# Attention scores as three products of split operands, with one scaling moved from VectorE to ScalarE

## What is computed

```python
o_a = natten_latent(qa, ka, va, ka_c, va_c, rpb_a[l])    # 8 heads of 64, with a bias, "A"
o_b = swa_latent(qb, kb, vb, kb_c, vb_c, sink_b[l])      # 12 heads of 64, banded, with a sink, "B"
o_c = mla_latent(qc, kc, vc, kc_c, vc_c)                 # 6 heads of 128+64, dense, "C"
x = x + gate * merge_out(o_a, o_b, o_c, z, w_out[l])
if not last:                                             # layer 0 only: the context stream
    oa_c, ob_c, oc_c = ctx_attn(...), ctx_attn(...), ctx_attn(...)
    xc = xc + gate_c * merge_out(oa_c, ob_c, oc_c, z_c, w_out[l])
```

## Time and profile before

| | |
|---|---|
| median of three runs | 3156.88 us (3156.69 to 3157.13) |
| the profiled execution | 3160.49 us, its span 3159.2 us |
| TensorE busy | 3093.2 us (98%) |
| VectorE busy | 1893.5 us (60%) |
| ScalarE busy | 1340.6 us (42%) |
| GpSimd busy | 295.6 us (9%) |
| attention of layer 0 | about 692 to 850 us |
| attention of layer 1 | about 1488 to 1584 us |

### The profile page before, as it was taken

How to read it: one execution, slowest core, us unless ns; L and a number is a source line. 1 busy time by engine, 2 the same in 40 slices (tenths; PEclk the granted TensorE clock), 3 DMA queues, 4 the chain that set the end, 5 groups by cost and what they waited for, 6 DMA issues and landing times.

```text
span 3159.2 us, 51244 instructions
## 1 busy us (share of the span) xinstructions
PE 3093.2 (98%) x21274; PEld 2759.7 (87%) x21274; DVE 1893.5 (60%) x2949; ACT 1340.6 (42%) x2075; POOL 295.6 (9%) x386
## 2 busy tenths in 40 slices
PE   7999999999999999998999999999999999999998
PEld 3788888875688898886599999999999999999998
DVE  4376676377768566446757755555556555555445
ACT  4422333355532643345544444344444444444443
POOL 0001000017421010002710000000000000000000
PEclk9999999999999999999999999999999999999999
DMA  9776554221166387432064555555554555555554
GB/s 398 290 236 217 180 192 161 79 74 67 41 253 220 121 300 245 154 112 103 31 204 167 180 184 186 185 190 194 191 193 166 199 194 194 193 195 194 194 194 160
DMA packets 154984, 571.27 MB, mean 181 GB/s; under 512 B 17760, under 2 KB 17888, under 8 KB 152192
## 3 DMA queue, kind: packets, MB, share of 16 engines
q1 hardware_dynamic: 147312, 533.71, 49.2%
q0 software_dynamic: 7440, 34.28, 3.0%
HBM read 555.34 MB, written 12.58 MB: 180 GB/s over the span
## 4 chain that ended last, share of the span: by engine, by line
PE 92%; DVE 2%; DMA 2%; ACT 2%; issue 1%; POOL 1%; SPq 0%; DVEq 0%; ACTq 0%
PE ps L908 20%; PE ps L910 20%; PE ps L909 20%; PE ps L897 7%; PE ps L899 7%; PE ps L898 7%; DMA sb_raw<-in_stream 2%; PE ps L1081 2%; PE ps L1039 1%; PE ps L1062 1%; PE ps L817 1%; PE ps L1055 1%; POOL sb_p L2258 1%; PE ps L1030 1%; DVE sb_p L1982 1%
## 5 line engine op out<-in xcount | busy, mean ns | idle before, releaser
L1566 DVE TENSOR_TENSOR sb_wlo<-sb_raw,sb_whi 128x1024 fp32r<-128x1024 f32 (+1 forms) x809 | 983.5, 1217 | 974.9 <-ACT sb_whi L1151 973.3
L1151 ACT ACTIVATE sb_whi<-sb_raw 128x1024 fp32r<-128x1024 f32 (+1 forms) x813 | 853.9, 1051 | 1030.5 <-PE ps L910 781.0
L908 PE MATMUL ps<-sb_hn_hi,sb_whi 128*128 128x256 f32 (+4 forms) x2944 | 822.3, 279 | 4.4 <-DVE sb_hn_lo L1680 4.4
L909 PE MATMUL ps<-sb_hn_lo,sb_whi 128*128 128x256 f32 (+4 forms) x2944 | 820.9, 279 | 0.0
L910 PE MATMUL ps<-sb_hn_hi,sb_wlo 128*128 128x256 f32 (+4 forms) x2944 | 820.7, 279 | 0.0
L908 PEld LDWEIGHTS ps<-sb_hn_hi,sb_whi 128*128 128x128 f32 x2944 | 555.1, 189 | 5.2 <-DVE sb_hn_lo L1680 4.6
L910 PEld LDWEIGHTS ps<-sb_hn_hi,sb_wlo 128*128 128x128 f32 x2944 | 555.5, 189 | 0.0
L909 PEld LDWEIGHTS ps<-sb_hn_lo,sb_whi 128*128 128x128 f32 x2944 | 555.3, 189 | 0.0
L899 PE MATMUL ps<-sb_whi,sb_lo 128*128 128x512 f32 (+1 forms) x968 | 376.4, 389 | 0.0
L897 PE MATMUL ps<-sb_whi,sb_hi 128*128 128x512 f32 x896 | 356.0, 397 | 5.3 <-DVE sb_lo L1660 4.1
L898 PE MATMUL ps<-sb_wlo,sb_hi 128*128 128x512 f32 x896 | 350.0, 391 | 0.0
(11 more groups left out here) (306 smaller groups left out, 4270.2 us busy)
## 6 DMA issues: line engine op xcount, KB each, us to landing
sb_raw<-in_stream SPq DMA_DIRECT2D x939, 512.0 KB, 3.4
sb_T<-in_stream SPq DMA_DIRECT2D x41, 512.0 KB, 10.7
sb_raw<-in_stream SPq DMA_DIRECT2D x25, 384.0 KB, 3.0
sb_T<-in_x SPq DMA_DIRECT2D x4, 1024.0 KB, 9.4
z_scratch<-sb_scr POOLq DMA_DIRECT2D x16, 256.0 KB, 3.8
sb_zb<-z_scratch POOLq DMA_DIRECT2D x16, 256.0 KB, 3.0
sb_bias<-in_bias POOLq DMA_DIRECT2D x4, 1024.0 KB, 6.0
x_scratch<-sb_T POOLq DMA_DIRECT2D x4, 1024.0 KB, 4.5
```

The source lines that it names most:

```text
L908: PE.matmul(o, whi[:, s, w], xh, start=k == 0, stop=False)
L909: PE.matmul(o, whi[:, s, w], xl, start=False, stop=False)
L1151: AC.activation(whi[:, s, 0:width], raw_of(n)[:, 0:width], ACT.Copy).then_inc(*hi.up((g.id, c)))
L1566: VE.tensor_tensor(wlo[:, s, 0:width], raw_of(n)[:, 0:width], whi[:, s, 0:width].bitcast(F32), ALU.subtract).then_inc(*lo.up((g.id, c)))
```

## The change

The score products of eight units (B2, B3, B4, B5, A0, A1, A2, A3, the list `PAIRED`) are made of split operands. Their queries and keys are written as a rounded and a remaining part into slots of the ring `whi` and `wlo`, which are not used by weights in that stretch; the two `split` steps of chunks 0 and 1 of `wout` are therefore moved from unit 2 to the last unit, and wait until the last user of their slot has been scored. ScalarE writes the rounded parts (`operand_hi`, two instructions a unit) at the first slot of the unit ahead, and VectorE the remainders (`operand_lo`, two instructions) at the second slot of the unit ahead, after its part of `att`. TensorE waits for the latter before the unit's first score. The scaling of head 0 goes, for all 78 slots, from VectorE to ScalarE, where it stands between the exponentials of slot s and the copy of slot s-2.

```diff
+PAIRED = [u for u, (kind, tile) in enumerate(UNITS) if kind == "A" or kind == "B" and tile > 1]
...
+            ahead, first = slots[s].unit + 1, s == 0 or slots[s - 1].unit < slots[s].unit
+            if ahead in PAIRED and first:
+                pl.add("operand_hi", l, ahead)
+            if ahead in PAIRED and not first and slots[s - 1].qt == 0 and slots[s].stream == 0:
+                pl.add("operand_lo", l, ahead)
-            if slots[s].unit == 2 and slots[s].stream == 0:
+            if slots[s].unit == PAIRED[-1] and slots[s].stream == 0:
                 pl.split()
...
+    def operands(l, u):
+        s = (third_first[l].m0 + PAIRED.index(u) + 1 - len(PAIRED) + 2) % RING
+        n, (kind, tile) = L if l else 2 * L, UNITS[u]
+        q, k = (T_QA + tile, T_KA + tile) if kind == "A" else (T_QB + tile, T_KB + tile // 3)
+        return ((T[:, q, 0:n], whi[:, s, 0:n], wlo[:, s, 0:n]),
+                (T[:, k, :], whi[:, s, 512:1024], wlo[:, s, 512:1024]))
...
+            elif t.unit in PAIRED:
+                if t.stream == 0 and t.qt == 0:
+                    PE.wait_ge(*v_ev.at("operand_lo", l, t.unit))
+                (_, qh, ql), (_, kh, kl) = operands(l, t.unit)
+                for i, (q, k) in enumerate(((qh, kh), (qh, kl), (ql, kh))):
+                    for h in range(2):
+                        mm = PE.matmul(out[h], q[half[h], qs], k[half[h], ks], start=i == 0, stop=i == 2,
+                                       tile_position=(64 * h, 0))
...
+            if g.kind == "wout" and g.index == 0 and c < RING:
+                AC.wait_ge(*last_scored(g.layer, PAIRED[c - RING]))
...
+        def operand_hi(l, u):
+            j = PAIRED.index(u)
+            AC.wait_ge(*(last_scored(l, PAIRED[j - RING]) if j >= RING else used.at("done", pl.keys[l].id)))
+            for v, hi_, _ in operands(l, u):
+                ins = AC.activation(hi_, v, ACT.Copy)
...
+            if 1 <= s <= len(slots):
+                AC.wait_ge(*v_ev.at("sums", l, s - 1))
+                p_ = p_of(slots[s - 1], 0)
+                AC.activation(p_, p_, ACT.Copy, scale=stat[:, (s - 1) % 4, 2, 0:1]).then_inc(*normed.up((l, s - 1)))
...
+        def operand_lo(l, u):
+            VE.wait_ge(*a_ev.at("operand_hi", l, u))
+            for v, hi_, lo_ in operands(l, u):
+                ins = VE.tensor_tensor(lo_, v, hi_.bitcast(F32), ALU.subtract)
...
-                VE.wait_ge(*v_ev.last())
-                p_ = p_of(t, 0)
-                VE.tensor_scalar(p_, p_, st_[:, 2, 0:1], None, ALU.mult).then_inc(*normed.up((l, s - 1)))
```

More of the change, by code:

```diff
@@ L650, in key_nope, with last_scored @@
         return HF[:, head, :]
+    def operands(l, u):
[4 more added lines that the diff above has]
+                (T[:, k, :], whi[:, s, 512:1024], wlo[:, s, 512:1024]))
+    def last_scored(l, u):
+        return scored.at(l, max(t.s for t in slots_of(l) if t.unit == u), 1)
+    third_first = [next(g for g in pl.groups if g.kind == "wout" and g.layer == l) for l in range(DEPTH)]
     def query_rope(tile):
@@ L1035, in score @@
                         *scored.up((l, s, h)))
+            elif t.unit in PAIRED:
[6 more added lines that the diff above has]
+                                       tile_position=(64 * h, 0))
+                        if i == 2:
+                            mm.then_inc(*scored.up((l, s, h)))
             else:
-                q, k = (T_QA + t.tile, T_KA + t.tile) if t.kind == "A" else (T_QB + t.tile, T_KB + t.tile // 3)
+                q, k = T_QB + t.tile, T_KB + t.tile // 3
                 for h in range(2):
@@ L1462, in score @@
                 AC.activation(p_, p_, ACT.Exp, bias=st_[:, 0, h:h + 1], scale=-1.0, accum_out=st_[:, 1, h:h + 1]).then_inc(*exped.up((l, s, h)))
+        def operand_hi(l, u):
[3 more added lines that the diff above has]
+                ins = AC.activation(hi_, v, ACT.Copy)
+            ins.then_inc(*a_ev.up(("operand_hi", l, u)))
         def att(l, slots, s):
+            if 1 <= s <= len(slots):
+                AC.wait_ge(*v_ev.at("sums", l, s - 1))
+                p_ = p_of(slots[s - 1], 0)
+                AC.activation(p_, p_, ACT.Copy, scale=stat[:, (s - 1) % 4, 2, 0:1]).then_inc(*normed.up((l, s - 1)))
             if 2 <= s < len(slots) + 2:
@@ L1521, in scalar_engine @@
                 latent_roots(st[1])
+            elif st[0] == "operand_hi":
+                operand_hi(*st[1:])
             elif st[0] == "key_square":
@@ L1983, in score @@
                                         ALU.add, ALU.min, stat[:, s % 4, 0, h:h + 1]).then_inc(*maxed.up((l, s, h)))
+        def operand_lo(l, u):
+            VE.wait_ge(*a_ev.at("operand_hi", l, u))
+            for v, hi_, lo_ in operands(l, u):
+                ins = VE.tensor_tensor(lo_, v, hi_.bitcast(F32), ALU.subtract)
+            ins.then_inc(*v_ev.up(("operand_lo", l, u)))
         def att(l, slots, s):
@@ L2061, in vector_engine @@
                 VE.tensor_tensor(rq[:, :, 0], rq[:, :, 0], rq[:, :, 1], ALU.add).then_inc(*v_ev.up(("rq_sum", st[1])))
+            elif st[0] == "operand_lo":
+                operand_lo(*st[1:])
             elif st[0] == "key_square":
```

## The result

| | before | after |
|---|---|---|
| median | 3157.01 us (3156.69 to 3158.66, 4 runs) | 3188.32 us (3187.11 to 3197.34, 4 runs) |
| ratio of the medians | | 1.0098 [1.0063, 1.0133] |
| profiled execution, its span | 3160.49, 3159.2 us | 3188.18, 3186.8 us |
| first score to first values behind chunk 0, layer 0 | 163.93 us | 175.14 us |
| the same in layer 1 | 105.19 us | 121.93 us |

The kernel became slower by 31.3 us, where +16.7 was forecast; the range ended at 3186. The spans differ by 27.6 us and the medians by 3.7 more, since the profiled execution of before lay 3.5 above its median. The last two rows of the table are read from the timelines: they run from the first score of a layer's attention to the first products with the values after chunk 0 of `wout`.

A forecast was written before the change was run, and what follows sets the result against it. The prediction took TensorE to bound attention. Layer 1 without its end +9.3, layer 0 without its end +3.7 and the two ends +3.7 gave +16.7 us, 3173.6 on the median of 3156.9; range 3158 to 3186.

The forecast's parts named there:

- both mechanisms: TensorE waits for VectorE's remainders before scores in layer 1, and for ScalarE's scaling before transposes in layer 0.
- The two rivals that ended at or under 3167: All added work hidden, 3150 to 3153 us, 8%; or half of it hidden, 3158 to 3167 us, 20%.
- the one in which the two heads run one after the other: Float32r score pairs take 1.58 us, not 0.87; 28 us more, 3195 to 3202 us, 7%.
- the score products: TensorE's score pairs get shorter, saving 3.0 us in layer 1 and 4.3 in layer 0, 7.3 together.
- layer 1 without its end: Eight TensorE waits for remainders, 14.3 us, less 3.0 for scores and 2 of old idle time: +9.3 us.
- The 2 us of old idle time: Layer 1: TensorE's existing idle time taken to fall together with the new stalls, 2 us (bounds 0 and 3.3).
- layer 0 without its end: Scaling behind the exponentials delays transposes: five units +4.0, two units -0.5, B0 and B1 +0.2, sum +3.7 us.
- the two ends: Late splits of chunks 0 and 1 delay last scores and first chunk: +2.4 layer 1, +1.3 layer 0, together +3.7.
- the second rival: Half is hidden, new waits replace old idle time and layer 0 comes out even: +9, say 3163 us, 20%.
- the first rival: All added work is hidden and the score products pay: 3150 to 3153 us, 8%.

The follow-up runs named there:

- the scaling alone: The kernel before with only the scaling of head 0 moved from VectorE to ScalarE: 3171.25 us, 1.0024 [0.9993, 1.0056].
- The late splits alone: The kernel before with only the splits of chunks 0 and 1 moved from unit C0 to the last unit: 3167.04 us, 1.001 [0.998, 1.004].
- the run with the remainders earlier: The kernel after with VectorE's remainders moved between its reciprocals and the copy of the turned head: 3177.46 us, 1.0052 [1.0019, 1.0085].
- six units: Kernel before with split scores for B2 to B5, A0, A1, remainders before the copy, chunks 0 and 1 split around C0 and C2: 3158.64 us, 1.0001.

## Why the prediction was wrong

**Right: the direction and both mechanisms.** TensorE bounds attention, and what it waits for in either layer is what the forecast named. The two rivals that ended at or under 3167 are out, and so is the one in which the two heads run one after the other (0.90 us, not 1.58).

**Nearly right in size: the score products**, 0.90 and 0.55 us for a pair against 0.87 and 0.55.

**Right in its waits, short of one term: layer 1 without its end**, forecast +9.3. The first score of A3 came 13.3 us later, counted from the first score of the layer, and 13.5 counted from C0. Four of the eight waits are 1.70 or 1.71 us, and the two with the larger gate 2.03, as worked out (1.7 and 1.7 + 0.33). The other two are 2.43 and 2.31; there GpSimd was masking the bias beside the remainders (below). The eight are 15.6 us for 14.3. The 2 us of old idle time that I let fall together with them is borne out: the time in which TensorE stood grew by 13.0 and not by 15.6. The new products save 2.3 and not 3.0, since 14 pairs and not 16 lie ahead of the first score of A3, at some 0.16 each. What the forecast had at nothing is the clock, 2.9 us. 15.6 - 2.6 - 2.3 + 2.9 is 13.6.

**Right in sum, for reasons partly wrong: layer 0 without its end**, forecast +3.7. The first score of A3 came 3.9 us later. Here too the clock is in it and was in no term: it was at the lower level for 13.7 us ahead of A3, for 6.8 before. And the forecast charged the scaling only where a rounded part stood ahead of it, and the scaling alone costs 5.2 us in the layer, end included, with no such part in the kernel.

**The step that failed: the two ends, and the clock put at nothing.** The ends were forecast at +1.3 in layer 0 and +2.4 in layer 1. They are +7.3 and +3.5 (what is left of 11.2 and 16.7), 10.8 for 3.7, outside the bound of 7 too. By the rows above, TensorE stood 3.5 and 2.5 us longer in them, and was busy 3.8 and 1.0 us longer. For layer 0 the prediction names the splitting of y and the masks of the next slot as queued behind the two halves of the split, but shows no working for its +1.3, so which part of it failed can't be read from it. What the runs show in its place is a chain: VectorE's half waits 2.20 us for ScalarE's and stands ahead of the masks, and the moved scaling stands behind the exponentials. The late splits alone cost 4.2 us there, from C2 to the chunk, and the scaling alone 1.8. In layer 1 the like wait of TensorE is 3.91 us, with 1.3 before.

The longer busy time is the clock, of which no term of the sum speaks. At the end of layer 0 it is at 1.2 GHz from 849.26 to 862.92:

```profile
849.26:862.92 13.66, 10.02 (x40) 7.12 (x41) 7.41 (x24) 10.01 (x26) 4.98 (x4) 0.50 0.21 74
```

The same query over every part of the two stretches at that level says that TensorE was busy for 32.2 us of it, and for 12.8 before. At 2.9 us for the 6.8 of layer 1, as between after and the run with the remainders earlier, the 19.4 more come to some 8 us, which is an estimate. The ends have 13.4 of them, some 5.6 us. That is most of the 11.2 us by which attention lies above the forecast (27.9 for 16.7). The medians changed by 31.3 us; what that is above 27.9 comes from where the profiled executions lie among the others.

**Two slips of the prediction** that changed nothing: the sum of the second rival, +9, gives 3166 and not 3163, and the range of 3158 to 3186 leaves out all of the first rival, 3150 to 3153, and not its lower half.

**Which part costs what.** Layer 0: late splits 3.4, scaling 5.2, place of the remainders 1.8, together 10.4 of 11.2. Layer 1: place of the remainders 14.3, scaling 3.4, late splits -1.0, together 16.7 of 16.7. The late splits and the scaling are read against the kernel before and the place of the remainders against the kernel after, so they need not add: with the scaling taken back from the whole change layer 1 gained nothing. That they add up is luck: without the first column they are 8.9 for 10.9 in layer 0 and 18.4 for 17.0 in layer 1.

**The price of what the change is for.** Placed as well as I could, split scores of six units lose 0.9 us in layer 1 against plain ones, and in layer 0 0.2 without the first column. With better places for the last remainders they might come out even in layer 1; that wasn't tried.

## What to carry to other kernels

When every engine walks one written list, the price of an added instruction is where it stands: the same 16 remainders of layer 1 cost 14 us more behind the copy of the turned head than ahead of it, where VectorE waited anyway. Some 3 of the 14 are the clock, which fell behind the waits. Of a step that has a half on each of two engines, follow both, and at the end of a phase above all, because there nothing is left to hide behind. And look at where steps of this kind stand already: moving two old splits by a few instructions took 2.6 us off attention, and the faster products, net of making their operands, took nothing off it.

## What the runs showed of the hardware

- **GpSimd beside VectorE.** With the scaling of head 0 moved to ScalarE and nothing else changed, GpSimd's 26 scalings of a head in layer 1 took 1.55 to 1.58 us; in the kernel before 19 of the 26 took 1.84 to 1.86. So VectorE's scaling lengthens them. Beside VectorE's remainders it went either way. Here are one pair with the remainders earlier, which cost neither engine anything, and one with six units, which lengthened both (1.43 us for 1.02, and 2.11 for 1.85):

```profile
1546.61 1.56 POOL L2314 TENSOR_SCALAR sb_p<-sb_p,sb_stat 128x512 f32<-128x512 f32 x1 [0.33 <-DVE sb_stat L2041]
1547.55 1.03 DVE L2033 TENSOR_TENSOR sb_wlo<-sb_T,sb_whi 128x256 fp32r<-128x256 f32 x2 [1.04 <-ACT sb_whi L1500]
...
1494.60 2.11 POOL L2315 TENSOR_SCALAR sb_p<-sb_p,sb_stat 128x512 f32<-128x512 f32 x1 [1.02 <-DVE sb_stat L2040]
1494.94 1.43 DVE L2032 TENSOR_TENSOR sb_wlo<-sb_T,sb_whi 128x256 fp32r<-128x256 f32 x2
```

 With six units two scalings that began 0.1 us behind such a pair took 2.26 and 2.27, and the pairs their usual time. What decides isn't shown. In the kernel after VectorE was slowed by GpSimd's product of two SBUF operands:

```profile
1538.64 1.59 POOL L2257 TENSOR_TENSOR sb_bias<-sb_bias,sb_const 128x256 f32<-128x256 f32 x2
...
1539.03 1.75 DVE L2032 TENSOR_TENSOR sb_wlo<-sb_T,sb_whi 128x256 fp32r<-128x256 f32 x2
...
1540.93 0.50 PE L1061 MATMUL ps<-sb_whi 64*128 64x512 f32 x2 [2.43 <-DVE sb_wlo L2032]
```

 The pair of remainders took 1.75 us and not 1.02. The Trainium skill (SBUF — State Buffer, Summary: rules for kernel authors) says that of such two the second blocks until the first finishes. VectorE's pair began 0.39 us behind GpSimd's and was 0.73 longer, less than if it had stood still until GpSimd's pair ended at 1540.23; since each pair is two instructions, a block until the end of GpSimd's first is not excluded. For a scaling on GpSimd in the first place and a remainder in the second, and the first pair above show no block, and the second pair shows 0.41 us.

- **The clock falls behind waits of this size.** It went to 0.50 within a wait of 3.51 us and stayed there until 862.92. Behind waits of 1.7 to 2.4 us it was at that level for 3.4 us (1521.69 to 1525.10, 1542.17 to 1545.58, and 791.24 to 794.65, behind one of 2.02), but not behind each of them. A stall can therefore cost more than its length. The Trainium skill (TensorE: Matmul & The Clock Gate, What's actually happening) has the two levels, and the trace agrees: the transposes of a slot took 1.97 us at one and 1.09 at the other.

- **One pace is not the same in every execution.** The part behind attention took from 1573.9 to 1615.4 us in profiles of kernels that are alike there, at a granted clock of 1.00 for nearly all of it, with the same kind of product at a mean of 276 ns in the short ones and 281 in the long. I don't know why.
